# One decoder step, two layers: in the first head of a layer, the order of the low parts, the squares' sums, the norm sums and the turning of queries and keys

## The chip, the cores and the metric

The kernel runs on one core of a Trainium2 chip. The metric is the device time of one execution in microseconds (us); the figure of a kernel is the median of its runs. TensorE (PE) multiplies matrices into PSUM, VectorE (DVE) and ScalarE (ACT) work on SBUF and PSUM, GpSimd (POOL) works on SBUF, and SyncE (SP) here issues the transfers of the weights. The engines run side by side and wait for one another on semaphores.

## The reference, cut to what matters

A prompt of 512 tokens and a group of 8 single-token samples go through the same two layers; the kernel puts them side by side as 520 columns.

```python
def rmsnorm(x, g):
    y = xf * lax.rsqrt(jnp.mean(xf * xf, axis=-1, keepdims=True) + EPS)
    return (y * g.astype(jnp.float32)).astype(x.dtype)

def rope(x, pos):                       # turning by the position
    x1, x2 = x[..., :half], x[..., half:]
    return jnp.concatenate([x1 * cos - x2 * sin, x1 * sin + x2 * cos], axis=-1)

def layer(x, pos, S_ret, ...):
    h = rmsnorm(x, norm_mix)
    proj = h @ w_in
    q, k, v, g_ret, x_lru, y_lru, g_a, g_b = jnp.split(proj, IN_SPLITS, axis=-1)
    qf = rope(q..., pos)
    kf = rope(k..., pos) * (RET_DK ** -0.5)
    o, S_new = retention(qf, kf, vf, S_ret)      # 4 heads, scores, states
    ...                                          # RG-LRU branch, merge, SwiGLU
```

The root of the mean square is one number per token. It scales a whole column of `h @ w_in`, so that the kernel multiplies the raw x (times the gain) by the weights and scales the products by the inverse root afterwards.

## The kernel before, in words

Channels lie on the 128 partitions and the 520 tokens along the free axis, as two halves of 260 columns. A weight tile of 1024x128 is a unit of 8 blocks. Each factor is split in two parts, high and low, and a product is three matmuls (high by high, low by high, high by low), for two halves: 6 matmuls a block and 48 a unit (`product`, the matmuls of L370). GpSimd makes the two parts of the weights (L356 high, L358 low), in halves of a unit, with two units in the buffer; SyncE loads a unit when the buffer is free.

A layer begins with its first head (`one_head(head, True)`), with every later head after it. TensorE's order in the first head is: the two query tiles together, block by block (`twin`, which waits for the low part of x of each block, `x_low_s`); the sums of the squares over the channels (`norm_sums`, L450, two matmuls that the trace shows as four, into two banks of the tensor aux); two key tiles into aux (`key_banks`); four value tiles into the two slots of the tensor proj (`whole`), with the reading of the samples' states (`read_begin`, which waits for the transfers of four states and for `qz_full`, and `read_out`, L555) inside the first value tile and at the end of the fourth; then the scores (L582), whose four tiles go into banks 0, 1, 2 and 0 of aux, the transposes, the first gate tile and the rest.

VectorE's order in the first layer's start: per block of x the low part (`first_low`, L797), then the addition of the block before's squares to SSQ (`first_square`, L804 and L806). ScalarE makes the high part (L1343) and the square (L1348) of a block in turn, with two buffers for the squares, so that the square of block m waits until VectorE added block m-2. In the second layer the low parts and the sums come from the last stage of the first layer. In both layers VectorE then waits for the root (ScalarE, L1370, after TensorE's sums), takes the reciprocal into RINV (L784), multiplies COS and SIN by it (L828, L829), and turns queries and keys with these scaled tables (L922, L923, L928, L929, then L934 and L936 in `turned`). `q_parts` (L912, then the copies of L944) ends with the signal `qz_full`. The values are scaled by RINV as they are read (L956).

`sq_sum` counts added squares, `sq_mm` TensorE's sums, `x_sd` roots, `t_free` tiles of proj that were read, `rope_done` turned tensors, `ro_done` readings of the states.

Of the kernel before, what the change touches and what calls it, by code (L numbers as in the profile page):

```python
# [133 lines left out]
def build(nc, wstream, xt, params, norms, tables, dec, kdt, slru, sconv, sret, ident,  # L134
          yt, ret_p, ret_s, lru_o, conv_p, conv_s, vscr):
    ctx = ExitStack()
    with ctx:
# [84 lines left out]
        SQT = fview(at["rt"], 2, TOK)  # L222
        LAM = sb("lambda_series", [P, 6, LT])
# [139 lines left out]
        def _(pe):  # L363
# [90 lines left out]
            AUX_SUMS = [AUX[:, c, 0:HALF] for c in range(2)]  # L454

# [6 lines left out]
            for layer in range(DEPTH):  # L462
# [48 lines left out]
                def one_head(head, first):  # L511
# [6 lines left out]
                    if first:  # L518
# [8 lines left out]
                        pe.wait_ge(s["sq_sum"], layer * (2 * MT) + MT)  # L527
                        norm_sums(AUX_SUMS, s["sq_mm"])
# [7 lines left out]
                    for i in range(KT, QK):  # L536
                        if first and i == QK - 1:
                            pe.wait_ge(s["x_sd"], layer + 1)
                        whole(ub, i, tb, i, XH, XL, into=first_keys(i) if first else None)

# [19 lines left out]
                    if first:  # L560
                        for i in range(VT):
                            whole(ub, uv + i, tb, v0 + i, XH, XL,
                                  midway=lambda: read_begin(i // 3) if i in (0, 3) else None,
                                  freed_by=tb + (i + 1) if i < 2 else None,
                                  middle=MT // 2 if i else MT - 1)
                            if i in (0, 3):
                                read_out(i // 3)
# [209 lines left out]
        def _(dve):  # L777
# [22 lines left out]
            def first_square(m):  # L800

                dve.wait_ge(s["sq_full"], m + 1)
                if m == 0:
                    ts(SSQ, SQT[:, 0, :], 1.0, None, ALU.mult).then_inc(s["sq_sum"], 1)  # L804
                else:
                    tt(SSQ, SSQ, SQT[:, m % 2, :], ALU.add).then_inc(s["sq_sum"], 1)  # L806
                dve.drain()  # L807

            first_low(0)
            for m in range(1, MT):  # L810
                first_low(m)
                first_square(m - 1)
            first_square(MT - 1)
# [4 lines left out]
            with dve.Fori(0, DEPTH) as layer:  # L818
# [5 lines left out]
                dve.wait_ge(s["x_sd"], layer + 1)  # L824
                root_inverse(RINV[:])
                dve.drain()
                dve.wait_ge(s["trig_ld"], layer * 32 + 32)
                tt(COS[:], COS[:], RINV[:], ALU.mult)  # L828
                tt(SIN[:], SIN[:], RINV[:], ALU.mult)  # L829
# [73 lines left out]
                def one_head(head, first):  # L903
# [26 lines left out]

                    def turned(dst, between):
# [26 lines left out]

                    turn_even(0, QF)
                    turn_odd(1)  # L960
                    if first:
                        dve.wait_ge(s["sfin_st"], hh * 16 + 16)
                        turn_even(KT, KF)
                        turned(QF, lambda: None)
                        turn_odd(KT + 1)
                        q_parts()
                        turned(KF, lambda: None)
                        dve.tensor_copy(GNC[:], CUR[:, bass.ds(head * VT + PC_GN, VT)])
                        key_low()
                        value(0)  # L970
# [3 lines left out]
                        value(1)  # L974
# [352 lines left out]
        def _(act):  # L1327
# [17 lines left out]
            def first_square(m):  # L1345
                if m >= 2:
                    act.wait_ge(s["sq_sum"], m - 1)
                A(SQT[:, m % 2, :], X[:, m, :], ACT.Square).then_inc(s["sq_full"], 1)  # L1348

# [7 lines left out]
            first_high(0)  # L1357
            for m in range(1, MT):
                first_high(m)
                first_square(m - 1)  # L1360
                if m == 1:
                    act.dma_start(ID[:], ident).then_inc(s["setup_ld"], 16)
                    act.dma_start(KDT[:], kdt).then_inc(s["setup_ld"], 16)
                    act.dma_start(PAR[:], params).then_inc(s["setup_ld"], 16)
            first_square(MT - 1)

            def norm_root(n):

                act.wait_ge(s["sq_mm"], n)
                A(halves(RINV[:]), AUX[:, 0:2, 0:HALF], ACT.Sqrt, bias=EPST, scale=1.0 / DM  # L1370
# [480 lines left out]
```

## Time and profile before

| | |
|---|---|
| median of 3 runs | 2459.19 us (2458.72 to 2462.03) |
| the profiled execution's own time | 2456.01 us |
| its span | 2454.2 us |
| TensorE busy | 2423.3 us, 99% |
| GpSimd busy | 1634.4 us, 67% |
| VectorE busy | 1178.2 us, 48% |
| ScalarE busy | 645.1 us, 26% |
| first product, layer 0 | starts at 7.95 us |
| first product, layer 1 | starts at 1226.79 us |

The span runs from the first to the last instruction. Since TensorE is nearly always busy, a change can only bring what TensorE waits somewhere, or cost what it makes TensorE wait.

### The profile page before, as it was taken

How to read it: one execution, taken by the hardware profiler on the slowest of the kernel's cores; microseconds unless marked ns; L12 is line 12 of the kernel's file. 1: busy time of each engine (PE TensorE's matmuls, PEld its weight loads, DVE VectorE, ACT ScalarE, POOL GpSimd, SP SyncE). 2: the span in 40 equal slices, each digit the busy share in tenths (PEclk: the TensorE clock that was granted, in tenths of full speed). 3: DMA queues.
4: the chain of work that ended last, by engine and by line, in shares of the span. 5: the costliest groups of instructions: out<-in, count | busy, mean ns of one | idle time of the engine just before them, and what ended most of it. 6: DMA issues, size and time to landing. Idle time of an engine off the chain costs nothing.

```text
span 2454.2 us, 53114 instructions
## 1 busy us (share of the span) xinstructions
PE 2423.3 (99%) x19640; PEld 2364.6 (96%) x19640; DVE 1178.2 (48%) x1587; ACT 645.1 (26%) x982; POOL 1634.4 (67%) x1685
## 2 busy tenths in 40 slices
PE   8999999999999999999999999999999999999998
PEld 7999999999999999999999999999999999999998
DVE  8646363678644432022266373736786454211223
ACT  2404040446811211011114041413666112100111
POOL 6464646578887776776765555555888776667765
PEclk9999999999999999999999999999999999999999
DMA  5636363522232222322257373645223232223222
GB/s 209 237 121 244 121 241 117 206 87 91 85 102 92 95 90 81 104 90 83 94 166 250 114 250 120 239 133 190 88 91 90 97 95 91 90 82 103 91 85 88
DMA packets 121737, 315.51 MB, mean 129 GB/s; under 512 B 12192, under 2 KB 12960, under 8 KB 121568
## 3 DMA queue, kind: packets, MB, share of 16 engines
q1 hardware_dynamic: 60480, 199.78, 25.5%
q10 hardware_dynamic: 61088, 113.34, 13.0%
q8 instruction: 123, 2.02, 0.3%
q14 instruction: 46, 0.38, 0.0%
HBM read 272.69 MB, written 40.38 MB: 128 GB/s over the span
## 4 chain that ended last, share of the span: by engine, by line
PE 91%; DVE 4%; DVEq 2%; ACT 1%; issue 1%; DMA 0%; ACTq 0%
PE proj L370 55%; PE aux L370 27%; PE aux L625 2%; DVE scratch L1126 2%; PE aux L582 1%; PE aux L555 1%; PE proj L633 1%; PE aux L633 1%; DVEq L1129 1%; DVE scratch L1184 1%; PE aux L611 1%; PE proj L625 0%; DVEq L807 0%; DVEq L1160 0%; DVEq L1187 0%
## 5 line engine op out<-in xcount | busy, mean ns | idle before, releaser
L358 POOL TENSOR_TENSOR w_low<-w_raw,w_high 128x512 fp32r<-128x512 f32 x840 | 1091.1, 1299 | 124.5 <-issue 2.1
L356 POOL TENSOR_SCALAR w_high<-w_raw 128x512 fp32r<-128x512 f32 x840 | 549.7, 654 | 674.1 <-PE proj L370 495.4
L370 PE MATMUL proj<-x_high,w_high 128*128 128x260 f32 x2752 | 558.8, 284 | 11.4 <-DVE x_low L797 11.0
L370 PE MATMUL proj<-x_high,w_low 128*128 128x260 f32 x2752 | 555.0, 283 | 0.0
L370 PE MATMUL proj<-x_low,w_high 128*128 128x260 f32 x2752 | 554.1, 283 | 0.0
L370 PEld LDWEIGHTS proj<-x_high,w_high 128*128 128x128 f32 x2752 | 425.3, 189 | 20.6 <-issue 16.9
L370 PEld LDWEIGHTS proj<-x_high,w_low 128*128 128x128 f32 x2752 | 424.8, 189 | 0.0
L370 PEld LDWEIGHTS proj<-x_low,w_high 128*128 128x128 f32 x2752 | 424.0, 189 | 0.0
L370 PE MATMUL proj<-split_scratch,w_high 128*128 128x260 f32 x2544 | 409.2, 283 | 0.0
L370 PEld LDWEIGHTS proj<-split_scratch,w_high 128*128 128x128 f32 x2544 | 348.6, 188 | 5.0 <-issue 5.0
L370 PE MATMUL aux<-x_high,w_high 128*128 128x260 f32 x1344 | 270.9, 283 | 0.0
L370 PE MATMUL aux<-x_high,w_low 128*128 128x260 f32 x1344 | 270.7, 283 | 0.0
L370 PE MATMUL aux<-x_low,w_high 128*128 128x260 f32 x1344 | 270.2, 283 | 0.0
L370 PE MATMUL proj<-split_scratch,w_low 128*128 128x260 f32 x1272 | 255.9, 282 | 0.0
L370 PE MATMUL aux<-split_scratch,w_high 128*128 128x260 f32 x1456 | 233.7, 282 | 5.6 <-ACT scratch L1557 5.6
L370 PEld LDWEIGHTS aux<-x_high,w_high 128*128 128x128 f32 x1344 | 207.2, 188 | 0.1
L370 PEld LDWEIGHTS aux<-x_high,w_low 128*128 128x128 f32 x1344 | 207.1, 188 | 0.0
L370 PEld LDWEIGHTS aux<-x_low,w_high 128*128 128x128 f32 x1344 | 206.7, 188 | 0.0
L370 PEld LDWEIGHTS aux<-split_scratch,w_high 128*128 128x128 f32 x1456 | 199.4, 188 | 6.0 <-POOL w_low L358 6.0
L370 PEld LDWEIGHTS proj<-split_scratch,w_low 128*128 128x128 f32 x1272 | 196.0, 188 | 0.0
L370 PE MATMUL aux<-split_scratch,w_low 128*128 128x260 f32 x728 | 146.4, 282 | 0.0
L370 PEld LDWEIGHTS aux<-split_scratch,w_low 128*128 128x128 f32 x728 | 112.2, 188 | 0.0
(197 smaller groups left out, 2283.5 us busy)
## 6 DMA issues: line engine op xcount, KB each, us to landing
w_raw<-in_wstream SPq DMA_DIRECT2D x252, 512.0 KB, 3.5
scratch<-in_sret ACTq DMA_DIRECT2D x96, 512.0 KB, 6.9
out_ret_s<-scratch ACTq DMA_DIRECT2D x64, 512.0 KB, 4.4
w_raw<-in_wstream SPq DMA_DIRECT2D x72, 448.0 KB, 3.3
w_raw<-in_wstream SPq DMA_DIRECT2D x48, 384.0 KB, 3.0
scratch<-v_rows ACTq DMA_DIRECT2D x64, 256.0 KB, 3.9
w_raw<-in_wstream SPq DMA_DIRECT2D x48, 320.0 KB, 2.9
out_ret_p<-scratch ACTq DMA_DIRECT2D x8, 512.0 KB, 5.5
```

Of the source, the lines that this page charges most:

```text
L356: pool.tensor_scalar(WH[:, j, w], WR[:, j, w], 1.0, 0.0, ALU.mult, ALU.add)
L358: pool.tensor_tensor(WL[:, j, w], WR[:, j, w], WH[:, j, w].bitcast(F32), ALU.subtract).then_inc(s["w_split"], 1)
L370: m = pe.matmul(out, wt[:, w, blk * P:(blk + 1) * P], x[xi], start=first and n == 0, stop=last and n == 2)
L555: m = pe.matmul(AUX[QUAD * r:QUAD * (r + 1), BANK["RO"], :], QZ[:, d, SRING * n + r, :], SS[r][:, d, :], start=n == d == 0, stop=n == NBAT ...
L582: m = pe.matmul(aux(f"SC{j}")[:, 0:SEQ - j * P], a[:, d, j * P:(j + 1) * P], b[:, d, j * P:SEQ], start=d == n == 0, stop=d == KT - 1 and n ...
L611: m = pe.transpose(aux(f"TV{j}")[:, e * P:(e + 1) * P], VF[:, e, j * P:(j + 1) * P], ID[:])
L625: m = pe.matmul(aux(f"AT{t}"), a[:, w], b[:, j, :], start=j == n == 0, stop=j == t and n == 2)
L633: m = pe.matmul(aux(f"ST{d}"), a[:, j, d * P:(d + 1) * P], b[:, j, :], start=j == n == 0, stop=j == TT - 1 and n == 2)
L1126: m = stt(XCF[:, t, d:SEQ], xr[:, 0:SEQ - d], CUR[:, PC_CW + c * CW + j:PC_CW + c * CW + j + 1], XCF[:, t, d:SEQ], ALU.mult, ALU.add)
L1129: dve.drain()
L1184: dve.tensor_tensor_scan(HF[:, 0:SEQ], AF[:, b, 0:SEQ], IX[:, b, 0:SEQ], 0.0, ALU.mult, ALU.add)
```

## The change

It touches the start of both layers, on three engines.

- ScalarE (first layer only): all eight high parts first, then the three small transfers, then all eight squares, into eight buffers of their own (SQ8, in a part of the scratch that the values use later) without a wait.
- VectorE (first layer only): all eight low parts, then all eight additions of squares.
- TensorE (both layers): the sums of the squares stand behind the two key tiles, in the second slot of proj. They wait there for `t_free` of both query tiles, since that slot held the second one. The first value tile then follows in the first slot. The reading of the first four states stands at the end of the second value tile, and no longer at that of the first. The second half of the reading begins at the last block of the fourth value tile, not at its middle.
- VectorE (both layers): queries are turned with the plain COS and SIN before the root is there (`turned_first`), then the keys' products with the tables; then the wait for the root and the reciprocal (`first_root`), the scaling of the turned queries by RINV (`scaled`, one instruction of 1040 elements), the last two steps of the keys and their scaling, the first value tile, and then `q_parts`. COS and SIN are scaled behind `key_low`, for the heads to come. The series for lambda is no longer parted by a value tile in its first half.

```diff
+        SQ8 = fview(at["vo"], MT, TOK)
...
-                        pe.wait_ge(s["sq_sum"], layer * (2 * MT) + MT)
-                        norm_sums(AUX_SUMS, s["sq_mm"])
                         pe.wait_ge(r_free[3], layer * USES[3] + 1)
...
                     for i in range(KT, QK):
-                        if first and i == QK - 1:
-                            pe.wait_ge(s["x_sd"], layer + 1)
                         whole(ub, i, tb, i, XH, XL, into=first_keys(i) if first else None)
+                    if first:
+                        pe.wait_ge(s["t_free"], tb + 2)
+                        pe.wait_ge(s["sq_sum"], layer * (2 * MT) + MT)
+                        norm_sums([PP[:, slot(1), c, 0:HALF] for c in range(2)], s["sq_mm"])
...
                         for i in range(VT):
+                            if i == 1:
+                                pe.wait_ge(s["x_sd"], layer + 1)
                             whole(ub, uv + i, tb, v0 + i, XH, XL,
-                                  midway=lambda: read_begin(i // 3) if i in (0, 3) else None,
-                                  freed_by=tb + (i + 1) if i < 2 else None,
-                                  middle=MT // 2 if i else MT - 1)
-                            if i in (0, 3):
+                                  midway=lambda: read_begin(i // 3) if i in (1, 3) else None,
+                                  freed_by=tb + (i + 1) if i < 2 else None, middle=MT - 1)
+                            if i in (1, 3):
                                 read_out(i // 3)
...
-            first_low(0)
-            for m in range(1, MT):
+            for m in range(MT):
                 first_low(m)
-                first_square(m - 1)
-            first_square(MT - 1)
+            for m in range(MT):
+                first_square(m)
...
-                dve.wait_ge(s["x_sd"], layer + 1)
-                root_inverse(RINV[:])
-                dve.drain()
-                dve.wait_ge(s["trig_ld"], layer * 32 + 32)
-                tt(COS[:], COS[:], RINV[:], ALU.mult)
-                tt(SIN[:], SIN[:], RINV[:], ALU.mult)
+                def first_root():
+
+                    dve.wait_ge(s["x_sd"], layer + 1)
+                    root_inverse(RINV[:])
+                    dve.drain()
...
+                    def turned_first(dst):
+
+                        dve.drain()
+                        tt(dst[:, 0, :], dst[:, 0, :], RT[:, 0, :], ALU.subtract)
+                        tt(dst[:, 1, :], dst[:, 1, :], RT[:, 1, :], ALU.add)
+                        dve.drain()
+
+                    def scaled(dst):
+
+                        tt(dst, dst, RINV[:].unsqueeze(1).broadcast_to([P, KT, TOK]), ALU.mult
+                           ).then_inc(s["rope_done"], 1)
+                        dve.drain()
...
                     turn_even(0, QF)
                     turn_odd(1)
                     if first:
+                        turned_first(QF)
                         dve.wait_ge(s["sfin_st"], hh * 16 + 16)
                         turn_even(KT, KF)
-                        turned(QF, lambda: None)
                         turn_odd(KT + 1)
+                        first_root()
+                        scaled(QF)
+                        turned_first(KF)
+                        scaled(KF)
+                        value(0)
                         q_parts()
-                        turned(KF, lambda: None)
                         dve.tensor_copy(GNC[:], CUR[:, bass.ds(head * VT + PC_GN, VT)])
                         key_low()
-                        value(0)
+                        value(1)
+                        tt(COS[:], COS[:], RINV[:], ALU.mult)
+                        tt(SIN[:], SIN[:], RINV[:], ALU.mult)
                         series_begin()
                         for n in (17, 15, 13):
                             series(n)
-                        value(1)
                         for n in (11, 9, 7):
                             series(n)
                         value(2)
...
             def first_square(m):
-                if m >= 2:
-                    act.wait_ge(s["sq_sum"], m - 1)
-                A(SQT[:, m % 2, :], X[:, m, :], ACT.Square).then_inc(s["sq_full"], 1)
+                A(SQ8[:, m, :], X[:, m, :], ACT.Square).then_inc(s["sq_full"], 1)
...
-            first_high(0)
-            for m in range(1, MT):
+            for m in range(MT):
                 first_high(m)
-                first_square(m - 1)
-                if m == 1:
...
+            for m in range(MT):
+                first_square(m)
...
-                A(halves(RINV[:]), AUX[:, 0:2, 0:HALF], ACT.Sqrt, bias=EPST, scale=1.0 / DM
+                A(halves(RINV[:]), PP[:, slot(1), :, 0:HALF], ACT.Sqrt, bias=EPST, scale=1.0 / DM
```

On VectorE, at the start of the first layer, the order before is (x_low is the low part of x, scratch holds squares and their sum):

```order
L797 SCALAR_TENSOR_TENSOR x_low<-residual,gain_cur,x_high 128x520 [waits x_high_s] x2
L804 TENSOR_SCALAR scratch<-scratch 128x520 [waits sq_full]
L797 SCALAR_TENSOR_TENSOR x_low<-residual,gain_cur,x_high 128x520 [waits x_high_s]
L806 TENSOR_TENSOR scratch<-scratch 128x520 [waits sq_full]
L797 SCALAR_TENSOR_TENSOR x_low<-residual,gain_cur,x_high 128x520 [waits x_high_s]
...
L797 SCALAR_TENSOR_TENSOR x_low<-residual,gain_cur,x_high 128x520 [waits x_high_s]
L806 TENSOR_TENSOR scratch<-scratch 128x520 [waits sq_full] x2
```

And now:

```order
L799 SCALAR_TENSOR_TENSOR x_low<-residual,gain_cur,x_high 128x520 [waits x_high_s] x8
L806 TENSOR_SCALAR scratch<-scratch 128x520 [waits sq_full]
L808 TENSOR_TENSOR scratch<-scratch 128x520 [waits sq_full] x7
L817 COPY rows_picked<-ident_sb 128x4 [waits setup_ld]
L817 COPY rows_picked<-ident_sb 128x4
```

The same sixteen instructions stand there; the six low parts that stood behind a sum now stand ahead of all sums.

On VectorE, between the root and the signal `qz_full`, which comes with the last copies into q_columns, the order before is (rinv is the inverse root, scratch holds queries, keys and values):

```order
L784 RECIPROCAL rinv<-rinv 128x520 [waits x_sd]
...
L828 TENSOR_TENSOR cos_r<-cos_r,rinv 128x520 [waits trig_ld]
L829 TENSOR_TENSOR sin_r<-sin_r,rinv 128x520
...
L934 TENSOR_TENSOR scratch<-scratch 128x520
L936 TENSOR_TENSOR scratch<-scratch 128x520
L781 REGISTER_ALU
L928 TENSOR_TENSOR scratch<-aux,sin_r 128x520 [waits p_done]
L929 TENSOR_TENSOR scratch<-aux,cos_r 128x520
L911 ISA
L912 SCALAR_TENSOR_TENSOR split_scratch<-scratch,split_scratch 128x1040 [waits qk_high]
L944 COPY q_columns<-scratch 128x2x4 x2
```

And now:

```order
L929 TENSOR_TENSOR scratch<-aux,cos_r 128x520
L827 REGISTER_ALU
L786 RECIPROCAL rinv<-rinv 128x520 [waits x_sd]
L940 TENSOR_TENSOR scratch<-scratch,rinv 128x1040
L934 TENSOR_TENSOR scratch<-scratch 128x520
L935 TENSOR_TENSOR scratch<-scratch 128x520
L940 TENSOR_TENSOR scratch<-scratch,rinv 128x1040
L783 REGISTER_ALU
L969 TENSOR_TENSOR scratch<-proj,rinv 128x520 [waits p_done]
L911 ISA
L912 SCALAR_TENSOR_TENSOR split_scratch<-scratch,split_scratch 128x1040 [waits qk_high]
L957 COPY q_columns<-scratch 128x2x4 x2
```

The products of queries and keys with the tables moved ahead of the reciprocal (L786); the keys' last two steps (L934, L935), two scalings (L940) and the first value tile (L969) now stand between the reciprocal and the copies.

On TensorE, around the sums, the order before is:

```order
L370 MATMUL proj<-x_high,w_low 128x260 x2
L450 MATMUL aux<-scratch,ones 128x260 [waits sq_sum,ring_free2]
L450 MATMUL aux<-scratch,ones 128x260
L370 MATMUL aux<-x_high,w_high 128x260 [waits w_split,ring_free3]
...
L370 MATMUL proj<-x_high,w_high 128x260 [waits s_loaded1,s_loaded0,s_loaded2,aux_free3,s_loaded3,qz_full,t_free]
...
L555 MATMUL aux<-scratch,q_columns 32x512 x8
L370 MATMUL proj<-x_high,w_high 128x260 [waits t_free,w_split]
```

And now:

```order
L453 MATMUL proj<-scratch,ones 128x260 [waits sq_sum,t_free]
L453 MATMUL proj<-scratch,ones 128x260
L373 MATMUL proj<-x_high,w_high 128x260 [waits t_free,w_split]
...
L373 MATMUL proj<-x_high,w_high 128x260 [waits t_free,w_split,x_sd]
...
L373 MATMUL proj<-x_high,w_high 128x260 [waits s_loaded1,s_loaded0,s_loaded2,aux_free3,s_loaded3,qz_full,t_free]
...
L556 MATMUL aux<-scratch,q_columns 32x512 x8
```

The sums wait for both query tiles to be read as well as for the squares, and the wait for `qz_full` stands one value tile later, after the wait for `x_sd`.

## Rows read from the trace of the kernel before

**Rows 1.** The page: busy time, share of the span and instructions.

```profile
PE 2423.3 (99%) x19640; PEld 2364.6 (96%) x19640; DVE 1178.2 (48%) x1587; ACT 645.1 (26%) x982; POOL 1634.4 (67%) x1685
```

**Rows 2.** Waits of TensorE, 0 to 80 us: total us, times, longest.

```profile
PE proj L370 <- DVE x_low L797: 11.0, 4, 8.0
```

**Rows 3.** Timeline, TensorE, layer 0: start, us, what, count [idle before <- releaser].

```profile
12.83 0.40 PE L370 MATMUL proj<-x_high,w_high 128*128 128x260 f32 x2
...
17.20 0.48 PE L370 MATMUL proj<-x_high,w_high 128*128 128x260 f32 x2 [1.11 <-DVE x_low L797]
...
26.86 1.12 PE L450 MATMUL aux<-scratch,ones 128*128 128x260 f32 x4 [0.89 <-DVE scratch L806]
27.62 0.59 PE L370 MATMUL aux<-x_high,w_high 128*128 128x260 f32 x2
...
39.34 0.40 PE L370 MATMUL proj<-x_high,w_high 128*128 128x260 f32 x2
...
45.20 1.92 PE L555 MATMUL aux<-scratch,q_columns 128*32 128x512 f32 x16
...
66.37 4.02 PE L582 MATMUL aux<-split_scratch 128*128 128x512 f32 x24
```

**Rows 4.** Timeline, VectorE, layer 0.

```profile
8.37 0.76 DVE L797 SCALAR_TENSOR_TENSOR x_low<-residual,gain_cur,x_high 128x520 fp32r<-128x520 f32 x1 [0.57 <-ACT x_high L1343]
...
16.97 1.78 DVE L806 TENSOR_TENSOR scratch<-scratch 128x520 f32<-128x520 f32 x1
18.84 0.93 DVE L797 SCALAR_TENSOR_TENSOR x_low<-residual,gain_cur,x_high 128x520 fp32r<-128x520 f32 x1
...
28.74 3.40 DVE L784 RECIPROCAL rinv<-rinv 128x520 f32<-128x520 f32 x1 [1.30 <-ACT rinv L1370]
32.31 1.70 DVE L828 TENSOR_TENSOR cos_r<-cos_r,rinv 128x520 f32<-128x520 f32 x1 [0.16 <-issue]
...
35.03 0.69 DVE L922 TENSOR_TENSOR scratch<-proj,cos_r 128x520 f32<-128x520 f32 x1
35.64 0.68 DVE L923 TENSOR_TENSOR scratch<-proj,sin_r 128x520 f32<-128x520 f32 x1
...
41.87 1.64 DVE L912 SCALAR_TENSOR_TENSOR split_scratch<-scratch,split_scratch 128x1040 fp32r<-128x1040 f32 x1
43.61 0.47 DVE L944 COPY q_columns<-scratch 128x8 f32<-128x8 f32 x2
44.18 1.80 DVE L934 TENSOR_TENSOR scratch<-scratch 128x520 f32<-128x520 f32 x1
45.90 0.69 DVE L936 TENSOR_TENSOR scratch<-scratch 128x520 f32<-128x520 f32 x1
...
47.73 1.62 DVE L912 SCALAR_TENSOR_TENSOR split_scratch<-scratch,split_scratch 128x1040 fp32r<-128x1040 f32 x1 [0.80 <-ACT split_scratch L1419]
...
58.85 0.70 DVE L956 TENSOR_TENSOR scratch<-proj,rinv 128x520 f32<-128x520 f32 x1 [2.17 <-PE proj L370]
...
66.97 0.68 DVE L998 TENSOR_SCALAR scratch<-aux 128x512 f32<-128x512 f32 x1
68.06 0.69 DVE L1006 TENSOR_TENSOR scratch<-aux,decay 128x512 f32<-128x512 f32 x1 [0.40 <-PE aux L582]
```

**Rows 5.** Timeline, GpSimd, layer 0.

```profile
32.17 1.29 POOL L358 TENSOR_TENSOR w_low<-w_raw,w_high 128x512 fp32r<-128x512 f32 x1
```

**Rows 6.** Timeline, TensorE, layer 1.

```profile
1226.79 0.48 PE L370 MATMUL proj<-x_high,w_high 128*128 128x260 f32 x2 [0.16 <-issue]
...
1238.33 1.04 PE L450 MATMUL aux<-scratch,ones 128*128 128x260 f32 x4
...
1256.15 0.48 PE L370 MATMUL proj<-x_high,w_high 128*128 128x260 f32 x2 [0.20 <-issue]
```

**Rows 7.** Timeline, VectorE, layer 1.

```profile
1254.90 1.15 DVE L944 COPY q_columns<-scratch 128x8 f32<-128x8 f32 x2
```

**Rows 8.** The page, DMA issues: KB each, us from issue to landing.

```profile
scratch<-in_sret ACTq DMA_DIRECT2D x96, 512.0 KB, 6.9
```

More of the change, by code:

```diff
@@ L222, in build @@
         SQT = fview(at["rt"], 2, TOK)
+        SQ8 = fview(at["vo"], MT, TOK)
+        assert at["vo"] + MT * TOK == at["rt"]
         LAM = sb("lambda_series", [P, 6, LT])
@@ L452, in norm_sums @@
                 m.then_inc(signal, 1)
-            AUX_SUMS = [AUX[:, c, 0:HALF] for c in range(2)]
             pe.sem_inc(s["p_done"], TILE0)
@@ L803, in first_square @@
                 if m == 0:
-                    ts(SSQ, SQT[:, 0, :], 1.0, None, ALU.mult).then_inc(s["sq_sum"], 1)
+                    ts(SSQ, SQ8[:, 0, :], 1.0, None, ALU.mult).then_inc(s["sq_sum"], 1)
                 else:
-                    tt(SSQ, SSQ, SQT[:, m % 2, :], ALU.add).then_inc(s["sq_sum"], 1)
+                    tt(SSQ, SSQ, SQ8[:, m, :], ALU.add).then_inc(s["sq_sum"], 1)
                 dve.drain()
-            first_low(0)
-            for m in range(1, MT):
+            for m in range(MT):
                 first_low(m)
-                first_square(m - 1)
-            first_square(MT - 1)
+            for m in range(MT):
+                first_square(m)
             dve.wait_ge(s["setup_ld"], 16 * 3)
@@ L957, in value @@
                            ).then_inc(s["t_free"], 1)
+                    if first:
+                        dve.wait_ge(s["trig_ld"], layer * 32 + 32)
                     turn_even(0, QF)
@@ L1356, in _ @@
             act.wait_ge(s["boot"], 2)
-            first_high(0)
-            for m in range(1, MT):
+            for m in range(MT):
                 first_high(m)
-                first_square(m - 1)
-                if m == 1:
[L1362 to L1365, printed above, removed]
+            act.dma_start(ID[:], ident).then_inc(s["setup_ld"], 16)
+            act.dma_start(KDT[:], kdt).then_inc(s["setup_ld"], 16)
+            act.dma_start(PAR[:], params).then_inc(s["setup_ld"], 16)
+            for m in range(MT):
+                first_square(m)
             def norm_root(n):
                 act.wait_ge(s["sq_mm"], n)
-                A(halves(RINV[:]), AUX[:, 0:2, 0:HALF], ACT.Sqrt, bias=EPST, scale=1.0 / DM
+                A(halves(RINV[:]), PP[:, slot(1), :, 0:HALF], ACT.Sqrt, bias=EPST, scale=1.0 / DM
                   ).then_inc(s["x_sd"], 1)
```

## The prediction, made before the changed kernel was run

> **What bounds the kernel now.** I read the page's busy times first: TensorE is busy for 99% of the span [rows 1], so a change counts by what TensorE waits before it and after it, and by nothing else. Then TensorE's waits of the first 80 us: four on VectorE's low parts, 11.0 us in all, of which 8.0 is the start of the kernel, where the first low part is made [rows 2]. The change doesn't touch that one. Then TensorE's timeline of that stretch. The third block of the two query tiles starts at 12.83, the sums at 26.86 [rows 3]. In layer 1 the whole pair of tiles takes 1238.33 - 1226.79 = 11.54 us for eight blocks, 1.44 us each, with hardly a wait [rows 6]. Six blocks from 12.83 would end at 12.83 + 8.65 = 21.5, so layer 0 loses 26.86 - 21.5 = 5.4 us here. VectorE's timeline tells why: the sum at 16.97 takes 1.78 us, and only at 18.84 does the next low part start [rows 4]. A low part waits behind a sum each time, and ScalarE's next high part behind the square that waited for that sum.
>
> Last I followed VectorE behind the sums, since TensorE comes back to it for `qz_full`. In layer 0 the copies end at 43.61 + 0.47 = 44.1 [rows 4], and TensorE reaches the reading at 45.20 without a wait [rows 3]. In layer 1 the copies end at 1254.90 + 1.15 = 1256.05 [rows 7] and TensorE goes on at 1256.15 [rows 6], where the sums' 0.76 us (27.62 - 26.86), two key tiles (11.72, 27.62 to 39.34) and seven blocks (5.05) from 1238.33 would give 1255.86 [rows 3, 6]: it waits 0.3 us. So this chain is on the edge today, and the change redraws it.
>
> **The stall that goes.** Of VectorE's sixteen instructions the two first low parts are done at 9.1 [rows 4]. Six low parts remain ahead of the sums. Even if each takes the sum's pace of 1.87 us (16.97 to 18.84), the eighth is there at 20.3, and its block is wanted at 21.5 - 1.44 = 20.1; at a low part's own 0.93 the eighth is there at 15. The high parts now wait for no sum. All 5.4 us go. Gain: 5.4 us, bounds 5.2 and 5.4. What is late next are the sums.
>
> **The sums in layer 0.** TensorE is ready for them after two key tiles of 11.72 us, at 21.5 + 11.7 = 33.2. They need all eight additions and both query tiles turned. Fourteen instructions from 9.1, at the present pace of a pair (1.87 for a sum, 0.93 for a low part, 2.8 together [rows 4]), take 7 x 2.8 = 19.6 us and end at 28.7; at 0.69 each (L923's kind) they would end at 19, at 1.87 each at 35. I take 28.7, since GpSimd, whose instructions stretch them, works without a pause there too. Small copies 0.7 (an estimate, the pair of L944 takes 0.47), four products of 0.61 from start to start (35.03 to 35.64) and 0.1 give 31.9: the sums start at 33.2, unhindered by 1.3 us.
>
> **VectorE's chain in layer 0.** From 31.9: the queries' two last steps, 2.4 (44.18 to 45.90 + 0.69), to 34.3; four products of the keys, 2.5 with their issue gaps, to 36.8. The root would be there at 33.2 + 1.9 = 35.1 (28.74 - 26.86), so VectorE itself is late now. Reciprocal 3.40 and the 0.17 to the next instruction [rows 4]: 40.4. Then five things stand ahead of the end of the copies. The scaling of 1040 elements is not in the trace; below it bounds twice 0.61 (1.2), above twice the stretched 1.70 (3.4), and I take the 1.64 of L912, which has two inputs in SBUF and as many elements: 42.0. The keys' last steps 2.5: 44.5. The second scaling 1.64 and a drain 0.1: 46.3. The value tile 0.7: 47.0. L912 1.64 and the copies 0.57: 49.2. TensorE wants them at 33.2 + 0.76 + 5.86 (39.34 to 45.20) + 5.05 = 44.9. It waits 4.3 us at the last block of the second value tile, with the reading, two value tiles and the scores behind it. Bounds: 0 (everything unstretched and VectorE on time for the root), and 7.6 (sums 2 us later, each later instruction 0.3 more).
>
> **The chain in layer 1.** Here queries are turned long before. From the start of the sums: 1.9 to the reciprocal, 3.6 through it, then 1.64 + 2.5 + 1.74 + 0.7 + 1.64 + 0.57, in all 14.3; TensorE comes after 0.76 + 5.86 + 5.05 = 11.7. It waits 2.6, less today's 0.3: loss 2.3 us, bounds -0.3 and 5.
>
> The stretching deserves a look, since three long instructions now stand in the chain. L828 started at 32.31, just behind GpSimd's product of 32.17, which took 1.29 us [rows 5], and ended at 34.01, 0.55 after it; L912 in 1.64 took only 0.4 more than twice 0.61 [rows 4]. The Trainium skill, SBUF — State Buffer, section Who interferes with whom, says that the port pair which VectorE and GpSimd share is an exclusive lock for the whole instruction, not a split of bandwidth. By that rule the 1040 elements cost at most one GpSimd instruction more; were it a split, they would stretch by L828's ratio to 3.4 us, and the four scalings of both layers would add some 7 us to the loss.
>
> **Behind the reading.** VectorE's work from the end of the copies to L998 took 66.97 - 44.08 = 22.9 us. Without the wait of 2.17 for TensorE, the 0.80 for ScalarE, the keys' last steps (2.4) and the first value tile (0.6), but with COS and SIN (1.70 + 0.6), it is 19.2 [rows 4]. TensorE needs one block, the reading, two value tiles and the reading: 0.72 + 1.9 + 11.5 + 1.9 = 16.1 [rows 3]. The first score tile is read 1.69 us behind that today (68.06 - 66.37), at 17.8; VectorE gets there at 19.2 + 0.6. The fourth score tile needs the first one's bank: it would start 3.6 us into the 3.95 of the scores, at 19.7, and the bank is free at 19.8 + 0.7 = 20.5. Loss 0.8 us in each layer, 1.6 in all, bounds 0 and 4. The gate tile behind it hides the rest.
>
> **Cost nothing.** The sums themselves move with their 0.76 us. ScalarE's transfers of four states start behind the root, as before: within 2 us of each other they land 6.9 us later (median) [rows 8], nearly 9 us after the root, and TensorE wants them 9.8 us after it. The second four have 10.8 us from the first reading (14.4 before). If that cover went, 1 to 2 us would come on top. The squares on ScalarE have eight buffers and wait for nothing. The later scaling of COS and SIN has the whole first head as cover. Nothing is moved past SyncE's or GpSimd's queues.
>
> **Sum.** -5.4 + 4.3 + 2.3 + 1.6 = +2.8 us. The profiled execution's own 2456.0 would be 2458.8; the median of the runs, 3.2 us above it, goes from 2459.2 to 2462.0.
>
> **Rivals.**
> - The gain stays: VectorE is at `qz_full` before TensorE in both layers. For it speaks that all bounds from below give a wait of nearly nothing; against it that in layer 1 today's chain, with its long instructions, was already 0.3 us late, and the new one has 14.3 us of work for 11.7. 5.4 + 0.3 = 5.7 us less: 2453.5.
> - Slower: the eight sums in a row are late themselves. If each of the fourteen instructions meets one of GpSimd's and takes nearer 1.7 than 1.4, the sums end at 33, the queries are turned at 36.2, and TensorE stands idle for 3.0 us behind the key tiles. VectorE then has 36.2 + 4.9 + 12.4 = 53.5 for the copies, TensorE comes at 36.2 + 11.7 = 47.9: 5.6 more. With layer 1 and the scores: -5.4 + 3.0 + 5.6 + 2.3 + 1.6 = +7.1, 2466.3. It decides from an end of the sums later than 30.0 on. For it speaks the 1.78 of the present sum, against it that pairs with a low part took 2.8.
> - The stall stays: the low parts are late by the transfers of x or by GpSimd's weight halves, which the same order speeds up no more. Then the sums start near 38, VectorE is ready in time, and only layer 1 and the scores cost: +2.3 + 0.8 and a part of the chain, 2463. Against it speaks that ScalarE waited for squares, and no longer for x, behind the second block.
>
> **Chances.** My forecast, a gain eaten by the wait for `qz_full` in both layers: 0.67. The gain stays: 0.13. The sums are late: 0.12. The stall stays: 0.08. A measurement of this kernel can tell about 0.2%, 4.9 us, from no change. Faster by that needs under 2454.3, more than half of the first rival: 0.08. Slower needs over 2464.1: most of the second rival and the upper part of my forecast, 0.18. Within it: 0.74. The range goes from 2455.5, where a third of the waits comes, to 2467, where the sums are late.
>
> **What would show it.** In the changed kernel's trace: no wait of TensorE on L799 behind the first; the sums' matmuls near 33.2; VectorE's reciprocal in layer 0 near 36.8, later than the root by more than 1 us; the copies into q_columns ending near 49 and a gap of TensorE of 4 us before the last block of the second value tile; a gap of 2.6 us there in layer 1, with the reciprocal 1.9 behind the sums; small gaps inside the scores. I am wrong if these gaps are absent, if the scaling L940 takes over 3 us, or if the time leaves the range.

## The result, and the profile after

The changed kernel has a median of 2464.10 us (8 runs, 2460.18 to 2467.58), the kernel before 2458.88 us (8 runs, 2454.38 to 2462.52) beside it: ratio 1.0021, 95% interval 1.0011 to 1.0030. It is slower by 5.2 us, in an interval of about 2.7 to 7.4 us. 2462.0 was forecast, with 2455.5 to 2467.0 as the range. All ratios here and below are of the fast runs, so that one run of e6 (9372 us) and one of the kernel before beside it (5006 us) are not in them. The profiled execution took 2462.75 us, its span is 2460.8 us, 6.6 above the span before. That span and the page's busy times are:

```profile
span 2460.8 us, 53120 instructions
...
PE 2428.0 (99%) x19640; PEld 2367.1 (96%) x19640; DVE 1186.6 (48%) x1591; ACT 644.6 (26%) x982; POOL 1637.0 (67%) x1685
```

TensorE is busy for 4.7 us more than in [rows 1] with as many instructions. So some of them ran longer, and not all of the loss is idle time. TensorE's waits from 0 to 120 us, against [rows 2]:

```profile
PE proj L373 <- DVE x_low L799: 8.1, 1, 8.1
PE proj L373 <- DVE q_columns L957: 4.4, 1, 4.4
PE proj L453 <- DVE scratch L929: 0.2, 1, 0.2
```

The three waits between blocks are gone, only the kernel's start is left on x_low; 4.4 us on the copies behind `qz_full` are new. TensorE's timeline of layer 0, against [rows 3]:

```profile
22.24 0.40 PE L373 MATMUL aux<-x_high,w_high 128*128 128x260 f32 x2
...
34.10 1.15 PE L453 MATMUL proj<-scratch,ones 128*128 128x260 f32 x4 [0.16 <-DVE scratch L929]
...
50.44 0.77 PE L373 MATMUL proj<-x_high,w_high 128*128 128x260 f32 x2 [4.38 <-DVE q_columns L957]
51.01 0.64 PE L373 MATMUL proj<-x_low,w_high 128*128 128x260 f32 x2
51.45 0.64 PE L373 MATMUL proj<-x_high,w_low 128*128 128x260 f32 x2
52.01 3.28 PE L556 MATMUL aux<-scratch,q_columns 128*32 128x512 f32 x16
55.22 0.51 PE L373 MATMUL proj<-x_high,w_high 128*128 128x260 f32 x2
```

The key tiles start at 22.24, so the two query tiles end 4.6 us earlier than 26.86. Behind the wait a pair of matmuls takes 0.44 us from start to start (51.01 to 51.45), not 0.24, and the reading 3.21 (52.01 to 55.22), not 1.85 (45.20 to 47.05 before). The windows of that stretch (busy times, then granted clock PEclk) show why. The first two are the wait and what follows, the last two the same in layer 1:

```profile
45.70:50.40 4.70, 0.36 (x4) 0.15 (x2) 4.37 (x9) 2.33 (x3) 1.19 (x1) 0.74 0.24 92
50.40:55.20 4.80, 4.76 (x22) 1.97 (x22) 3.96 (x12) 0.34 (x2) 0.00 (x0) 0.54 0.00 0
1265.50:1268.90 3.40, 0.12 (x2) 0.05 (x1) 3.23 (x7) 2.61 (x4) 1.69 (x2) 1.00 0.35 136
1268.90:1273.20 4.30, 4.30 (x22) 1.32 (x22) 3.93 (x12) 0.00 (x0) 0.00 (x0) 0.62 0.00 0
```

The granted clock is 0.54 right behind the wait, where TensorE works without a pause: nearly the lower of its two levels, 1.2 of 2.4 GHz. It had been idle for 4.4 us just before, and the 0.74 of the first window shows that the fall came inside that wait. In layer 1 the clock is 1.00 up to the end of the wait and 0.62 behind it, and the timeline, against [rows 6], shows the drop a moment later, inside the reading:

```profile
1253.73 1.04 PE L453 MATMUL proj<-scratch,ones 128*128 128x260 f32 x4
...
1268.88 0.48 PE L373 MATMUL proj<-x_high,w_high 128*128 128x260 f32 x2 [3.28 <-DVE q_columns L957]
...
1269.76 3.53 PE L556 MATMUL aux<-scratch,q_columns 128*32 128x512 f32 x16
1273.23 0.55 PE L373 MATMUL proj<-x_high,w_high 128*128 128x260 f32 x2
...
1284.86 0.48 PE L373 MATMUL proj<-x_high,w_high 128*128 128x260 f32 x2 [0.49 <-DMA scratch<-in_sret]
```

The last row is a new small wait, for the second four states. VectorE's timeline of layer 0, against [rows 4]:

```profile
19.45 9.79 DVE L808 TENSOR_TENSOR scratch<-scratch 128x520 f32<-128x520 f32 x7
...
29.99 1.25 DVE L824 COPY params_cur<-params_all 128x112 f32 x1 [0.18 <-issue]
...
31.53 0.70 DVE L922 TENSOR_TENSOR scratch<-proj,cos_r 128x520 f32<-128x520 f32 x1
...
38.14 3.39 DVE L786 RECIPROCAL rinv<-rinv 128x520 f32<-128x520 f32 x1
41.61 1.42 DVE L940 TENSOR_TENSOR scratch<-scratch,rinv 128x1040 f32<-128x1040 f32 x1
...
45.83 2.15 DVE L940 TENSOR_TENSOR scratch<-scratch,rinv 128x1040 f32<-128x1040 f32 x1
...
50.09 0.25 DVE L957 COPY q_columns<-scratch 128x8 f32<-128x8 f32 x2
...
50.39 1.23 DVE L912 SCALAR_TENSOR_TENSOR split_scratch<-scratch,split_scratch 128x1040 fp32r<-128x1040 f32 x1
...
61.29 0.70 DVE L969 TENSOR_TENSOR scratch<-proj,rinv 128x520 f32<-128x520 f32 x1 [1.73 <-PE proj L373]
```

The sums end at 29.2, the reciprocal starts at 38.1 without having waited for the root (which ended at 35.28 + 0.69), and the copies end at 50.3.

Where the 6.6 us of the two spans are: at the scores of layer 0 the changed kernel is 2.5 us behind (68.84 against 66.37). At the start of layer 1 it is 3.9 behind (1230.70 against 1226.79); the 1.4 between are a second stretch at the lower clock, behind a wait of 2.8 us for ScalarE that both kernels have (at 614 and 617 us) and that was followed by the lower clock in this execution and not in that of the kernel before. Layer 1 adds 5.4, to 9.3 at the scores (1287.59 against 1278.25). Later, at 1833 us, that same kind of wait was 0.6 us instead of 2.8 and gave 2.2 back, and the last stretch to the end gave 0.5. The +1.4 and -2.2 are taken as not the change's, since kernels that differ only elsewhere show them either way (that wait is 0.6 us in e1 below and 2.8 us in e2); the first head's 2.5 + 5.4 = 7.9 us are.

### The profile page after: what moved, and what is told of

Its sections match the earlier page's. It is cut to its first block, busy times and chain, and to the rows that moved or that the text cites. A ratio compares the mean times of both kernels' runs of the same rounds, so it can differ in the third digit from the quotient of the medians.

```text
span 2460.8 us, 53120 instructions
## 1 busy us (share of the span) xinstructions
PE 2428.0 (99%) x19640; PEld 2367.1 (96%) x19640; DVE 1186.6 (48%) x1591; ACT 644.6 (26%) x982; POOL 1637.0 (67%) x1685
## 4 chain that ended last, share of the span: by engine, by line
PE 89%; DVE 5%; DVEq 2%; ACT 2%; issue 1%; DMA 1%; ACTq 0%
PE proj L373 54%; PE aux L373 27%; PE aux L627 2%; DVE scratch L1146 2%; PE aux L556 1%; PE aux L584 1%; PE proj L635 1%; PE aux L635 1%; DVEq L1149 1%; DVE scratch L1204 1%; PE aux L613 1%; PE proj L627 0%; DMA scratch<-in_sret 0%; DVE scratch L808 0%; DVE x_low L799 0%
## 5 line engine op out<-in xcount | busy, mean ns | idle before, releaser
L359 POOL TENSOR_SCALAR w_high<-w_raw 128x512 fp32r<-128x512 f32 x840 | 555.6, 661 | 678.5 <-PE proj L373 509.5
L373 PE MATMUL proj<-x_high,w_high 128*128 128x260 f32 x2752 | 559.5, 284 | 16.3 <-DVE x_low L799 8.1
```

The source lines that it names most:

```text
L359: pool.tensor_scalar(WH[:, j, w], WR[:, j, w], 1.0, 0.0, ALU.mult, ALU.add)
L373: m = pe.matmul(out, wt[:, w, blk * P:(blk + 1) * P], x[xi], start=first and n == 0, stop=last and n == 2)
```

## The experiments

The theory after the comparison: TensorE waits for VectorE's order at `qz_full` in both layers, and pays the wait a second time in a stretch at the lower clock. The rivals: the lower clock has another cause; the start of layer 0 gained nothing that counts; and VectorE's sheer load, not its order, is the bound.

### The queries' parts first (e1)

```diff
                         scaled(QF)
+                        q_parts()
                         turned_first(KF)
                         scaled(KF)
                         value(0)
-                        q_parts()
```

> The changed kernel with q_parts (the low part of the queries and the copies that give qz_full) moved from behind the first value tile to right behind the scaling of the queries, ahead of the keys' last steps. Theory (TensorE waits for VectorE's order at qz_full, and its clock is halved for some us behind that wait): both waits (4.4 us in layer 0, 3.3 us in layer 1) and both stretches at the lower clock (about 2.1 and 1.6 us) go, so the median falls from 2464 to about 2453, below the kernel before by about 5. Rival 1 (the waits go but the clock is not tied to them): 2456 to 2457. Rival 2 (the wait moves on to the states' transfers or the value tiles): 2460 or more, with a wait of over 2 us on scratch<-in_sret or t_free.

Measured: 2460.93 us (11 runs), ratio to the kernel before 1.0005 (0.9996 to 1.0014). Both waits on q_columns are gone and the first reading takes 1.92 us in both layers. But the time is not to be told from that of the kernel before, 8 us over the 2453 of my theory: a miss. TensorE's waits from 0 to 80 us, and from 1240 to 1300 us:

```profile
PE proj L373 <- DVE x_low L799: 8.1, 1, 8.1
PE proj L373 <- DVE scratch L969: 1.5, 1, 1.5
PE aux L584 <- DVE scratch L1026: 1.0, 1, 1.0
PE proj L373 <- DMA scratch<-in_sret: 0.5, 1, 0.5
```

```profile
PE aux L584 <- DVE scratch L1026: 1.2, 1, 1.2
PE proj L373 <- DMA scratch<-in_sret: 0.7, 1, 0.7
```

Five smaller waits, 4.9 us in all, stand where the two large ones stood, on three releasers: the first value tile (L969, layer 0 only), which now comes behind `q_parts` and the keys; the scores' fourth tile, for the bank that VectorE reads (L1026); and the states' transfers. The value tile's and the transfers' are those of rival 2, though each is under its 2 us; its time, 2460 or more, came. What the 8 us hold beside these 4.9 is not shown.

### Matmuls of no use in place of the wait (e2)

```diff
                             if first:
                                 pe.wait_ge(s["t_free"], tb + (QK - 1))
+                                for _ in range(12 - 3 * layer):
+                                    pe.matmul(AUX[:, 3, 0:HALF], ONES[:], X[:, 0, 0:HALF], start=True, stop=True)
```

> The changed kernel in which TensorE, where it waits for qz_full, does matmuls of no use (12 in layer 0, 9 in layer 1, of ones by x into a free bank, about 0.38 us each) for about as long as the wait. Nothing else moves. Theory (the idle time brings the lower clock): the end of the second value tile is as late as in the changed kernel, but the blocks and the reading behind it run at the full clock, reading 1.9 us and not 3.2 to 3.5; the median falls by about 3.7 us, from 2464 to 2460. Rival (the lower clock has another cause, as the reading itself or the transfers): no change, 2464, granted clock of that stretch 0.7 as before.

Measured: 2462.98 us (11 runs), ratio 1.0014 (1.0005 to 1.0023). That is 1.7 us below the changed kernel by the ratios (1.0021), in intervals that overlap; the times alone don't decide, and the 2460 of the theory is missed by 3 us. The trace decides on the clock. TensorE's timeline of the place in layer 0, and windows from the end of the fill on, the first of layer 0 and the second of layer 1 (granted clock third from the end):

```profile
45.20 5.42 PE L548 MATMUL aux<-residual,ones 128*128 128x260 f32 x24
50.27 0.59 PE L373 MATMUL proj<-x_high,w_high 128*128 128x260 f32 x2
50.70 0.40 PE L373 MATMUL proj<-x_low,w_high 128*128 128x260 f32 x2
50.94 0.40 PE L373 MATMUL proj<-x_high,w_low 128*128 128x260 f32 x2
51.26 1.92 PE L558 MATMUL aux<-scratch,q_columns 128*32 128x512 f32 x16
```

```profile
50.00:54.80 4.80, 4.80 (x39) 3.14 (x38) 3.21 (x10) 0.00 (x0) 0.95 (x2) 1.00 0.07 18
...
1265.50:1270.00 4.50, 4.50 (x34) 2.75 (x34) 3.58 (x10) 0.18 (x1) 0.13 (x1) 1.00 0.01 4
```

TensorE goes on at 50.27, as late as the 50.44 of the changed kernel, but the clock is 1.00 and the reading takes 1.92 us in both layers, not 3.28 and 3.53. The second reading starts at 64.81 and no longer at 66.98. So idle time brought the lower clock, and the rival (the reading or the transfers as its cause) falls. That the median fell by less than forecast has a reason in the trace too. The fill was longer than the wait it replaced. VectorE's timeline in layer 0:

```profile
48.55 0.25 DVE L959 COPY q_columns<-scratch 128x8 f32<-128x8 f32 x2
...
64.92 0.70 DVE L971 TENSOR_TENSOR scratch<-proj,rinv 128x520 f32<-128x520 f32 x1 [0.86 <-PE proj L373]
```

The copies were done at 48.80, and TensorE was held until 50.27; in layer 1 until 1266.44, with the copies done at 1265.48. That is 2.5 us of the fill's own.

### The old start of layer 0 in the changed kernel (e3)

```diff
-            for m in range(MT):
+            first_low(0)
+            for m in range(1, MT):
                 first_low(m)
-            for m in range(MT):
-                first_square(m)
+                first_square(m - 1)
+            first_square(MT - 1)
```

(and ScalarE's loop likewise, with two buffers and its wait on `sq_sum`).

> The changed kernel with the start of layer 0 as in the kernel before (low parts and sums in turn, two buffers for the squares); all else stays. Theory (the new order removes 5.4 us at the two query tiles, but VectorE comes later to the root than TensorE's sums, so that part of it is waited again at qz_full): the three waits of about 1 us between blocks return, TensorE reaches the sums near 38, the wait at qz_full in layer 0 falls from 4.4 to about 3 us; the median is about 4 us above the changed kernel, 2468. Rival (the gain of the start was lost in full at qz_full): same as the changed kernel, 2464.

Measured: 2466.10 us (10 runs), ratio 1.0024 (1.0015 to 1.0034); against 1.0021 the 4 us are not seen in the times. In the trace the parts are there. TensorE's timeline:

```profile
17.33 0.48 PE L373 MATMUL proj<-x_high,w_high 128*128 128x260 f32 x2 [0.94 <-DVE x_low L799]
...
37.45 1.04 PE L453 MATMUL proj<-scratch,ones 128*128 128x260 f32 x4
...
52.55 0.48 PE L373 MATMUL proj<-x_high,w_high 128*128 128x260 f32 x2 [3.24 <-DVE q_columns L958]
53.44 3.02 PE L556 MATMUL aux<-scratch,q_columns 128*32 128x512 f32 x16
```

The sums start 3.4 us later than with the new start (37.45 against 34.10), the wait is 3.24 and not 4.38, and the scores' stretch is about 1.7 us later (second reading at 68.64 against 66.98). VectorE waited 0.3 us for the root here (reciprocal at 39.25). So of the 3.4 us that the new start gains, half is lost again: 1.1 in the longer wait at `qz_full`, since there VectorE is behind the root by 2 us, and 0.5 between TensorE's return and the second reading, where the clock was lower for longer (first reading 3.28 and not 3.02). It is between my theory's size and the rival.

### The new start alone (e4)

The edit is the change's on VectorE and ScalarE for layer 0 and its eight buffers, on the kernel before; TensorE's order and the later parts stay.

> The kernel before with only the start changed: all low parts ahead of all sums of squares, eight buffers, the matmuls of the sums where they stood, behind the two query tiles. Theory: the waits between blocks go, TensorE ends the two tiles near 21.5 and then waits for the last sum, which ends near 29 on VectorE as in the changed kernel: the sums start 2 to 3 us later than before and a stretch at the lower clock follows; median 2461 to 2464, slower than before by 2 to 5. Rival (without the interleaved low parts the sums end near 25 to 26): equal to before or up to 1 us faster.

Measured: 2460.45 us (11 runs), ratio 1.0006 (0.9997 to 1.0015): no difference that the times can tell, as the rival had it, not my 2 to 5 us. VectorE's and TensorE's timelines:

```profile
19.41 7.48 DVE L807 TENSOR_TENSOR scratch<-scratch 128x520 f32<-128x520 f32 x7
```

```profile
27.03 2.07 PE L451 MATMUL aux<-scratch,ones 128*128 128x260 f32 x4 [5.16 <-DVE scratch L807]
28.53 1.00 PE L371 MATMUL aux<-x_high,w_high 128*128 128x260 f32 x2
```

The seven sums take 7.5 us here against 9.8 in the changed kernel. The last four of them ran, in 0.70 us each, without a GpSimd instruction beside them: TensorE stood still, GpSimd got no free weight buffers and did nothing from 23.16 to 29.52. So the sums end at 26.9, nearer the rival's 25 to 26 than my 29; TensorE's sums start at 27.03, where they started before (26.86), behind one wait of 5.2 us that replaces four of about 1. The low parts' stall by itself was never worth 5.4 us: the last sum of squares was due at nearly the same time. A drop to the lower clock follows again (1.00 and not 0.59 for a pair), and the first reading starts at 47.05, 1.9 us later than the 45.20 of before; the interval of the times is too wide to show or exclude that.

### The root earlier in layer 1 (e5)

```diff
-                    for i in range(KT, QK):
-                        whole(...)
-                    if first:
-                        norm_sums(...)
+                    for i in range(KT, QK + 1):
+                        if first and i == QK - layer:
+                            norm_sums(...)       # with its two waits
+                        if i < QK:
+                            whole(...)
...
-                        turn_odd(KT + 1)
                         first_root()
                         scaled(QF)
+                        turn_odd(KT + 1)
                         q_parts()
```

> The kernel with q_parts moved up (e1), and two edits more: TensorE's sums stand between the two key tiles in layer 1 (behind both in layer 0, as before), and VectorE takes the reciprocal and scales the queries ahead of the second key tile's products. Theory (what was left in e1 are waits for work that stands behind the root: the states' transfers, 0.5 and 0.7 us, the first value tile, 1.5 us in layer 0, the scores' bank, 1.0 and 1.2 us): in layer 1 the root comes 5 us earlier, so that its two waits go (1.9 us); in layer 0, where VectorE itself is late, only the value tile's wait falls by about 1 us. Median about 3 us below e1, 2458. Rival (VectorE's load and not the root's place sets these waits): the wait on the scores' bank stays at 1 us in both layers, median 2460 to 2461.

Measured: 2456.39 us (11 runs), ratio 0.9993 (0.9984 to 1.0002), against 1.0005 of e1. From 1225 to 1300 us TensorE has no wait left, the scores' bank included, and in layer 0 these two stay, with two smaller ones (0.9 us ahead of the sums, for the turned queries, and 0.5 for the states' transfers):

```profile
50.45 0.47 PE L373 MATMUL proj<-x_high,w_high 128*128 128x260 f32 x2 [0.93 <-DVE scratch L970]
...
68.69 0.89 PE L585 MATMUL aux<-split_scratch 128*128 128x128 f32 x6 [1.14 <-DVE scratch L1027]
```

In layer 1, where TensorE's sums come a key tile earlier, the waits are gone; in layer 0, where only VectorE's order was changed, that for the bank stays as it was. So theory and rival hold for one layer each.

### Less on VectorE ahead of the scores, and transfers ahead of the root (e6, e7)

e6 is e5 with the first value tile right behind `q_parts`, and `state_terms()` moved to the end of the first head:

```diff
                         q_parts()
+                        value(0)
                         turned_first(KF)
                         scaled(KF)
-                        value(0)
...
-                        state_terms()
...
+                    if first:
+                        state_terms()
```

> As e5, and two edits more on VectorE: the first value tile is read right behind q_parts, and the conv state terms (six small instructions, 1.8 us) move from ahead of the scores to the end of the first head. Theory (VectorE's load between qz_full and the scores makes the scores' fourth tile wait): the waits on the first value tile and on the scores' bank go in both layers; median 1 to 3 us below e5, about 2456, which would be below the kernel before by some 3. Rival (the gain of the start is small by then and the lower clock at other waits decides): 2459, not to be told from the kernel before.

Measured: 2454.72 us (11 runs), ratio 0.9984 (0.9974 to 0.9993). The same kernel ran again beside e7:

> The same kernel as e6 once more, beside e7 on one chip. Expected: 0.9984 of the kernel before again, within 0.001, so that it is below the kernel before in both sets; if it was chance, 1.000.

Measured: 2453.63 us (11 runs), ratio 0.9982 (0.9973 to 0.9991), the same again and as expected. TensorE's waits that are left in the first head, in e6's first profile, all in layer 0:

```profile
PE proj L373 <- DMA scratch<-in_sret: 1.2, 1, 1.2
...
PE proj L453 <- DVE scratch L930: 0.6, 1, 0.6
PE aux L585 <- DVE scratch L1026: 0.4, 1, 0.4
```

The value tile's wait is gone, the scores' has fallen from 1.1 to 0.4, that for the transfers has grown from 0.5 to 1.2. In the profile of the second set the transfers' waits, 1.8 us in all, are the only ones left. e7 is e6 with the transfers of the decay table and of three of the four first states ahead of `norm_root` on ScalarE:

```diff
+                act.dma_start(DEC[:], dec[0:1]...).then_inc(s["dec_ld"], 16)
+                for r in range(SRING - 1):
+                    act.wait_ge(s_st[r], layer * (HEADS * 16 * SUSES[r]) + 16)
+                    act.dma_start(SS[r], sret[bass.ds(layer, 1), r, 0:1]...).then_inc(s_ld[r], 16)
                 norm_root(layer + 1)
```

> As e6, with ScalarE's transfers of the decay table and of the first three of the four states issued ahead of the root and no longer behind it (the fourth lands where the sum of squares lies and stays behind). Theory (in e6 TensorE's 1.2 us wait in layer 0 ahead of the first reading is for transfers that start only behind the root): the wait goes, the reading starts near 47.4 and the median is about 1 us below e6. Rival (the fourth state, still behind the root, sets the wait): the wait stays above 0.5 us and the median within 0.5 us of e6.

Measured: 2453.39 us (7 runs), ratio 0.9977 (0.9966 to 0.9988). Ahead of the first reading no wait is left (it starts at 45.63), and 0.3 us stand ahead of the second one, 0.4 at the scores' bank. The 1.0 us expected between e6 and e7 can't be told from the times, 0.9982 against 0.9977 with intervals that overlap. Both e6 and e7 beat the kernel before, by 4 to 5.6 us, and by the ratios the changed one. So VectorE's order set the two large waits; its load sets, at most, the small ones that are left in layer 0.

## Why the prediction was right, and where it was not

- **The stall that goes.** Right in kind: the waits between blocks vanished. TensorE reached the key tiles 5.4 us earlier by start (22.24 against 27.62), of which 0.76 is the moved sums: 4.6 and not 5.4. The rest went into the kernel's beginning, where the first matmuls run at the slow pace: it lasted until 13.84 us here and until 12.36 before, and between 12.3 and 14.3 in the other kernels' profiles, in no order of their starts. e4 shows that the stall was worth nothing that the times can tell by itself: 5.4 us was a gain only because the sums moved too.
- **The sums in layer 0.** The additions end at 29.2 for 28.7, queries turned at 34.05 for 31.9, TensorE held up for 0.2 us. The query products started at 31.5, behind small copies that took 2.2 us and not 0.7 (L824 alone took 1.25, and 0.22 in the kernel before).
- **The chain in layer 0.** Reciprocal at 38.1 for 36.8, copies done at 50.3 for 49.2, a wait of 4.4 for 4.3. The scalings took 1.42 and 2.15 us (1.64 taken), in layer 1 2.35 and 1.24: from the shortest to the longest 1.1 us, less than one of GpSimd's products (1.29), and no stretch to 3.4.
- **The chain in layer 1.** 1268.53 + 0.25 - 1253.73 = 15.05 us for 14.3 of work, a wait of 3.3 us for the 2.6 of the sum.
- **The step that failed** is "Behind the reading": 0.8 us in each layer for the scores' bank. It was nothing: TensorE waits for that bank in neither layer of the changed kernel, and VectorE waited for TensorE again (1.73 us at 61.29). What was mis-sized is VectorE's work from the copies to the first score tile, put at 19.2 us. From 50.34 to 69.44 it is 19.1 with 4.0 of waits for TensorE in it, so 15.1, and 15.2 in layer 1. The 19.2 was carried over from the kernel before, where these instructions stretched; behind the new wait GpSimd stood still (0.00 in the window from 50.40), and L912 took 1.23 us and not 1.62. The lower clock isn't what hides the wait: in e2, at the full clock, that work is 16.3 and 17.3 us, VectorE waits for TensorE (0.86 at 64.92), and the bank costs nothing either. e1 has waits of 1.0 and 1.2 us there, so the mechanism exists, with more work behind the copies: the keys' last steps, their scaling and the first value tile, 4.6 us in layer 0.
- **The term that was missing** is that clock: 50.44 to 55.22 is 4.78 us for what takes 1258.89 - 1256.15 = 2.74 at the full clock, 2.0 us; in layer 1 1268.88 to 1273.23, 1.6 us. I had no term for it. The first head as measured is -4.6 + 4.4 + 2.0 and 0.2 for the sums in layer 0, 2.0, where the starts say 2.5; and 3.3 + 1.6 + 0.5, less the present 0.3, in layer 1, 5.1, where the starts say 5.4. The 0.8 between belong to no wait that the traces show. Together 7.9 us, where I had 2.8. The median moved by 5.2, whose interval of 2.7 to 7.4 holds the forecast's +2.8 just. That the time lay in the range owes something to luck: 1.6 us too much for the bank stood against the missing 3.6 of the clock.
- **What is known of the clock.** The Trainium skill, TensorE: Matmul & The Clock Gate, Part 1: The HAM clock gate, says that the array runs at one of two clocks by how busy the engine has lately been. e2 agrees: with the wait filled the granted clock is 1.00 behind it, and 0.54 and 0.62 without.
- **Transfers at no cost.** Nearly: 0.5 us in layer 1, from the margin of 10.8 us that I named; in e1 0.5 and 0.7 ahead of the first reading too.
- **Rivals.** The gain doesn't stay, the sums were not late (29.2, and the point was 30.0), the stall did go. By the 4.9 us that the prediction took as the least that can be told from no change, 5.2 is just slower, and to that it gave 0.18. What the times can't show is the split of 5.2 us between the two layers; that is from single profiles, and the lower clock behind waits that no edit touched is worth 1 to 2 us in one execution and nothing in another.

## What to carry to other kernels

A wait between two engines that is removed in front is worth only what the next meeting point leaves: look at which work was due there anyway (here the last sum of squares, then `qz_full`), and walk the other engine's whole queue up to its signal. What feeds the signal goes ahead of what merely belongs to the same group. And where TensorE is nearly always busy, four waits of 1 us were cheaper than one of 4 to 5 us: the one cost a third to a half as much again in matmuls at the lower clock (2.0 us behind 4.4, 1.6 behind 3.3, some 1.7 behind 5.2 in e4), the four small ones nothing of the kind. This is read from single traces.

## What the runs showed of the hardware that was not expected

Behind waits of TensorE of 3.2 to 5.2 us the granted clock was at the lower level for 2.8 to 4.4 us in every profile that has one (five waits in the changed kernel, e3 and e4). It fell inside the wait in layer 0 of the changed kernel, and only 1 us behind TensorE's return in layer 1. Behind the waits of 2.8 us for ScalarE it fell in 7 of the 16 that the ten profiles have: in the changed kernel it was 0.72 there, before 1.00. These are windows of 6 us that begin half a us ahead of TensorE's return, of the changed kernel and of the one before:

```profile
616.50:622.50 6.00, 5.51 (x33) 5.54 (x34) 3.96 (x6) 4.60 (x7) 2.30 (x3) 0.72 0.21 59
```

```profile
614.00:620.00 6.00, 5.53 (x46) 5.56 (x47) 3.94 (x6) 4.60 (x7) 3.69 (x4) 1.00 0.20 59
```

33 matmul records against 46 in the same time. From that return to the start of layer 1 it is 1.4 us, more than some of the edits here are worth, and probably a part of the spread of 8 us between runs of one kernel. What decides which of the two happens stays open.

VectorE's instructions took longer beside a GpSimd at work: seven additions with two inputs in SBUF took 9.8 us beside it, and 7.5 us where TensorE's wait had stopped its supply of free buffers (e4). So a wait of TensorE changes VectorE's pace too, by way of GpSimd, and a duration read beside a busy GpSimd (the 19.2 us above) does not carry over to a stretch behind a wait. It is not only instructions with two inputs: the copy L824, with one, took 1.25 us in the changed kernel and 0.22 before.
